# The second tile's last 512 output columns go as two quarters in two PSUM banks, and the first batch's gathered columns in three

## The chip, the cores and the metric

The kernel runs on one core of a Trainium2 chip. A core has a matrix engine (TensorE, here PE, with its weight loads shown apart as PEld), a vector engine (DVE), a scalar engine (ACT), a general-purpose engine (GpSimd, here POOL), a sync engine (SP) that issues most DMAs, an on-chip memory (SBUF) and eight accumulation banks of 128 x 512 float32 (PSUM). Each engine runs its own instructions in the order written and waits for others on semaphores. The metric is the device time of one execution in microseconds. Before the change the median of three runs is 1198.57 us (1197.81 to 1199.47).

## The reference

Two layers over 256 tokens of width 1024, all in float32. Each layer is a mixer of three attentions with one output projection, and then a mixture of experts in which every token goes to 2 of 64 experts. Cut to what matters here:

```python
def reference(x, ...):
    for l in range(DEPTH):                                   # DEPTH = 2
        mix = hybrid_mixer(x, ...)                           # ..., return o @ w_out
        x = layer_norm(ALPHA * x + mix, ln1_g[l], ln1_b[l])
        ffn = moe_ffn(x, router_w, router_b, moe_w1[l], moe_w3[l], moe_w2[l])
        x = layer_norm(ALPHA * x + ffn, ln2_g[l], ln2_b[l])

def route(xf, router_w, router_b):                           # 64 experts in 8 groups of 8
    s = sigmoid(xf @ router_w); sb = s + router_b
    # the group with the largest sum of its best two, then its best two experts
    return e_idx, s_sel / s_sel.sum(-1, keepdims=True)

def moe_ffn(...):   # per expert e, over its tokens xb
    hb = silu(xb @ w1[e]) * (xb @ w3[e]);  y = hb @ w2[e]    # 1024 -> 256 -> 1024, gated sum per token
```

## The kernel before, in words

The 256 tokens are two tiles (t = 0, 1) of 128 rows; `x[:, t, :]` holds a tile. The experts are worked through in 16 batches of four, with 32 slots of tokens for each expert. The weights of all 64 experts are read in each layer, whatever the routing: 12 DMAs of 1 MB for a batch (two for w1 and w3 of each expert, `load_w13`, line 344, and one for w2, `load_w2`, line 348), into two sets of buffers, `w_even` and `w_odd`. SP issues them in written order and waits before each for the buffer's last reader. A w1/w3 buffer is free when the batch has multiplied it (`part_psum`, line 417), the four w2 buffers when the batch's second product is done (`y2_psum`, line 423 and line 431).

This case is about the stretch between the attention and the first batch, once in each layer. In order:

- PE multiplies the attention outputs `oT` by `w_out` (`out_chunk`, line 672): for tile t and half h of the 1024 columns eight matmuls of 512 columns into `mix_bank[t][h]` (banks 0 to 3), and `mix_psum` after the eighth.
- DVE adds each half to the residual and takes its statistics (`add_mix`, line 1141: a SCALAR_TENSOR_TENSOR at line 1144, BN_STATS at 1146), with the signal `z_ready`; `moments` (line 1148) closes the tile, POOL takes the power for the standard deviation (line 475).
- PE turns the sums around (`transpose_z`, line 570), ACT copies them to `xT` (`copy_xT`), and PE multiplies them by the router's weights (`route`, line 794).
- DVE selects the experts (`scores`, `select`, signal `picked`), PE counts ranks (lines 826 to 858), DVE places the tokens (`place`, line 1215, signal `chosen_ok`).
- PE gathers the normalised rows of the first batch by one-hot matmuls (`gather_first`, line 840): chunks 0 to 3 of eight into bank 2, 4 to 7 into bank 3. DVE copies bank 2 to `xg` with scale and offset (line 1277, four of 128 columns), ACT copies bank 3 (line 1513, four), and the first batch begins: for each expert k, PE multiplies chunks 0 to 3 after `xg_dve` and 4 to 7 after `xg_act` (lines 876 to 892). Expert 2 needs bank 0 back, so it waits for DVE's copy of expert 0 (line 1294, `part_dve`).
- Meanwhile the layer norm of x itself is finished: DVE does tile 0 by `center_first` (line 1156) and `stretch` (line 1165), one 512-column SCALAR_TENSOR_TENSOR per half each, with signal `x0_ready`; POOL does tile 1 in two multiplies and two adds (lines 519 and 523), with signal `x1_ready`, beginning after `routed`, DVE's last step of routing. ACT copies both to the banks `Y` (`seed`).

DVE, in written order around the gathered copies: `select(1)`, the stretch of half 0, `place(1)`, the number of rounds (lines 1268 to 1271), `weigh_scores(1)`, the stretch of half 1, the four copies of line 1277, `weights(1)` (lines 1205 to 1207), `weigh(0)` (lines 1233 and 1236), then the first batch.

Of the kernel before, what the change touches and what calls it, by code (L numbers as in the profile page):

```python
# [19 lines left out]
P = 128  # L20
# [59 lines left out]
def program(nc, a, consts, const_at, out):  # L80
# [17 lines left out]
    with ctx:  # L98
# [129 lines left out]
        class Signal:  # L228
# [23 lines left out]
        xT_psum, xT_dve, xT_act = Signal("xT_psum", 8), Signal("xT_dve", 3), Signal("xT_act", 7)  # L252
# [10 lines left out]
        mix_psum = Signal("mix_psum", 4)  # L263
# [5 lines left out]
            Signal("z_ready", 4), Signal("n_ready", 2), Signal("y_bits_set", 4), Signal("y_seeded", 4))  # L269
# [4 lines left out]
        chosen_ok, xg_dve, xg_act = Signal("chosen_ok"), Signal("xg_dve"), Signal("xg_act")  # L274
        gathered = Signal("gathered_first_half"), Signal("gathered_second_half")
# [47 lines left out]
        def _(sp):  # L323
# [3 lines left out]
            for l in range(DEPTH):  # L327
# [27 lines left out]
                if l == 0:  # L355
# [26 lines left out]
                sp.dma_start(router.rearrange("p (h c) e -> p h (c e)", h=2),  # L382
                             a["router_w"].rearrange("(h p c) e -> p h (c e)", h=2, c=4)).then_inc(router_in.sem, 16)
                sp.dma_start(router_bias, a["router_b"].partition_broadcast(P)).then_inc(router_in.sem, 16)
                for v, name in enumerate(("ln1_g", "ln1_b")):
                    sp.dma_start(g_cols[:, v, :], a[name].rearrange("l (p c) -> l p c", c=DC)[l]).then_inc(cols_in.sem, 16)
                    sp.dma_start(r_cols[:, v, :].rearrange("p (h c) -> p h c", h=2),
                                 a[name].rearrange("l (h p c) -> l p h c", h=2, c=4)[l]).then_inc(cols_in.sem, 16)
# [19 lines left out]
                after(sp, l, mix_psum, 4)  # L408
# [57 lines left out]
        def _(pool):  # L466
# [5 lines left out]
            for l in range(DEPTH):  # L472
# [65 lines left out]
        def _(pe):  # L538
# [16 lines left out]
            for l in range(DEPTH):  # L555
# [14 lines left out]
                def transpose_z(t, h):  # L570

                    after(pe, l, z_ready, 2 * t + h + 1)
                    zc = x[:, t, h * 512:(h + 1) * 512].rearrange("p (d c) -> p c d", c=4)
                    for c in range(4):
                        last = nc.tensor.transpose(bank[2 * t + h][:, c * P:(c + 1) * P], zc[:, c, :], ident)
                    last.then_inc(xT_psum.sem, 1)

# [216 lines left out]
                def route(t, h):  # L794
                    after(pe, l, xT_act, 3 + 2 * t + h + 1)
                    if t == 1 and h == 0:
                        after(pe, l, z_lin, 1)
                    for c in range(4 * h, 4 * h + 4):
                        last = mm(bank[0][:, t * NE:(t + 1) * NE], xT[:, c, t * P:(t + 1) * P], router[:, c, :],
                                  start=c == 0, stop=c == DC - 1)  # L800
                    if h == 1:
                        last.then_inc(z_psum.sem, 1)
# [9 lines left out]
                transpose_z(0, 0)  # L812
                transpose_z(0, 1)
# [7 lines left out]
                for c in range(5):  # L821
                    out_chunk(1, 1, c)
# [735 lines left out]
```

## Time and profile before

| | before |
|---|---|
| median of the runs | 1198.57 us |
| the profiled execution | 1198.07 us, span 1196.1 us |
| mean granted clock of TensorE | 0.986 |
| PE / PEld / DVE / ACT / POOL busy | 89% / 50% / 31% / 16% / 3% |
| chain that ended last, by engine | PE 47%; SPq 35%; DMA 8%; DVE 4%; issue 3%; ACT 1% |
| read from HBM | 441.16 MB, 370 GB/s over the span |

The page cuts the span into 40 equal slices of 29.9 us; a digit is the busy share in tenths:

```profile
PE   8999988899899888888899999899899889888885
DVE  2244462222232222122251535422232222222224
PEclk9999999999999999989999999999999999998998
DMA  9966389999999999999998456899999999999996
GB/s 353 345 222 246 141 322 420 420 420 420 421 421 421 420 421 421 421 420 420 396 350 319 149 216 245 338 418 421 421 421 421 421 421 420 420 420 421 421 420 235
```

Layer 0 fills slices 0 to 19, layer 1 the rest. The stretch of this case lies at 127 to 190 us, in slices 4 to 6, and at 717 to 780 us in layer 1. From there to the end of each layer DMA runs at one rate, 420 GB/s. A busy share is an average; what a change is worth is read from the waits at its place.

### The profile page before, as it was taken

How to read it: one execution, taken by the hardware profiler on the slowest of the kernel's cores; microseconds unless marked ns; L12 is line 12 of the kernel's file. 1: busy time of each engine (PE TensorE's matmuls, PEld its weight loads, DVE VectorE, ACT ScalarE, POOL GpSimd, SP SyncE). 2: the span in 40 equal slices, each digit the busy share in tenths (PEclk: the TensorE clock that was granted, in tenths of full speed). 3: DMA queues.
4: the chain of work that ended last, by engine and by line, in shares of the span. 5: the costliest groups of instructions: out<-in, count | busy, mean ns of one | idle time of the engine just before them, and what ended most of it. 6: DMA issues, size and time to landing. Idle time of an engine off the chain costs nothing.

```text
span 1196.1 us, 16270 instructions
## 1 busy us (share of the span) xinstructions
PE 1070.3 (89%) x6084; PEld 594.7 (50%) x6088; DVE 373.9 (31%) x1007; ACT 196.3 (16%) x469; POOL 34.0 (3%) x46
## 2 busy tenths in 40 slices
PE   8999988899899888888899999899899889888885
PEld 5565555444455444444356656544455444444442
DVE  2244462222232222122251535422232222222224
ACT  1144121111111111011122441211111111100110
POOL 0010020000000000000000100100000000000001
PEclk9999999999999999989999999999999999998998
DMA  9966389999999999999998456899999999999996
GB/s 353 345 222 246 141 322 420 420 420 420 421 421 421 420 421 421 421 420 420 396 350 319 149 216 245 338 418 421 421 421 421 421 421 420 420 420 421 421 420 235
DMA packets 85026, 442.68 MB, mean 370 GB/s; under 512 B 11009, under 2 KB 26497, under 8 KB 36865
## 3 DMA queue, kind: packets, MB, share of 16 engines
q1 hardware_dynamic: 84704, 441.60, 91.3%
q0 software_dynamic: 144, 0.58, 0.1%
q8 instruction: 20, 0.33, 0.1%
q14 instruction: 14, 0.11, 0.0%
q10 hardware_dynamic: 144, 0.07, 0.0%
HBM read 441.16 MB, written 1.05 MB: 370 GB/s over the span
## 4 chain that ended last, share of the span: by engine, by line
PE 47%; SPq 35%; DMA 8%; DVE 4%; issue 3%; ACT 1%; DVEq 0%; POOL 0%
SPq L344 24%; PE bank L602 12%; SPq L348 11%; PE bank L871 8%; PE bank L890 7%; DMA w_odd<-in_moe_w 7%; PE bank L680 5%; PE bank L922 4%; PE bank L927 4%; DMA w_odd<-in_w_in 2%; PE bank L897 1%; ACT moe L1366 1%; PE bank L650 1%; PE bank L665 1%; DVE moe L1320 1%
## 5 line engine op out<-in xcount | busy, mean ns | idle before, releaser
L871 PE MATMUL bank<-moe,x 128*128 128x128 f32 x960 | 233.1, 402 | 0.0
L871 PEld LDWEIGHTS bank<-moe,x 128*128 128x128 f32 x960 | 230.8, 335 | 0.0
L1366 ACT ACTIVATE moe<-bank 128x512 f32<-128x512 f32 (+2 forms) x190 | 101.4, 543 | 750.1 <-PE bank L890 361.0
L602 PE MATMUL bank<-w_odd 128*128 128x384 f32 (+1 forms) x448 | 150.9, 493 | 4.8 <-DMA w_odd<-in_w_in 2.9
L927 PE MATMUL bank<-moe 128*128 128x512 f32 x256 | 118.4, 605 | 24.1 <-DVE moe L1320 24.1
L890 PE MATMUL bank<-w_even,moe 128*32 128x512 f32 x1024 | 118.7, 609 | 17.1 <-DMA w_even<-in_moe_w 13.1
L890 PE MATMUL bank<-w_odd,moe 128*32 128x512 f32 x1024 | 118.0, 606 | 14.0 <-DMA w_odd<-in_moe_w 14.0
L1294 DVE COPY moe<-bank 128x512 f32<-128x512 f32 x64 | 44.2, 691 | 248.4 <-PE bank L890 248.1
L602 PEld LDWEIGHTS bank<-w_odd 128*128 128x128 f32 x448 | 83.6, 190 | 63.6 <-issue 14.2
L927 PEld LDWEIGHTS bank<-moe 128*128 128x128 f32 x256 | 46.0, 190 | 98.9 <-DVE moe L1320 51.4
L890 PEld LDWEIGHTS bank<-w_even,moe 128*32 128x32 f32 x1024 | 30.9, 111 | 100.0 <-issue 72.2
L890 PEld LDWEIGHTS bank<-w_odd,moe 128*32 128x32 f32 x1024 | 31.0, 111 | 95.7 <-issue 75.7
L922 PE MATMUL bank<-w_even,moe 128*32 128x512 f32 x512 | 58.3, 594 | 14.0 <-DVE moe L1311 14.0
L922 PE MATMUL bank<-w_odd,moe 128*32 128x512 f32 x480 | 54.8, 595 | 9.6 <-DVE moe L1311 9.6
L897 PE MATMUL bank<-moe,constants 128*32 128x512 f32 x256 | 35.8, 629 | 25.8 <-ACT moe L1366 25.8
L680 PE MATMUL bank<-w_odd 128*128 128x512 f32 x128 | 58.4, 599 | 0.0
L1305 DVE RECIPROCAL moe<-moe 128x256 f32<-128x256 f32 x32 | 56.1, 1753 | 1.1
L1320 DVE COPY moe<-bank 128x512 f32<-128x512 f32 x32 | 22.1, 692 | 109.3 <-PE bank L922 109.3
L1304 DVE TENSOR_SCALAR moe<-moe 128x256 f32<-128x256 f32 x32 | 9.4, 294 | 142.8 <-ACT moe L1525 142.8
L1366 ACT ACTIVATE w_odd<-bank 128x384 f32<-128x384 f32 (+3 forms) x74 | 32.5, 472 | 119.9 <-PE bank L602 34.5
L1311 DVE COPY moe<-bank 128x256 f32<-128x256 f32 x32 | 13.6, 425 | 101.6 <-PE bank L912 101.6
L922 PEld LDWEIGHTS bank<-w_even,moe 128*32 128x32 f32 x512 | 18.1, 109 | 42.7 <-issue 42.7
(160 smaller groups left out, 684.6 us busy)
## 6 DMA issues: line engine op xcount, KB each, us to landing
w_even<-in_moe_w SPq DMA_DIRECT2D x192, 1024.0 KB, 26.1
w_odd<-in_moe_w SPq DMA_DIRECT2D x184, 1024.0 KB, 26.4
w_odd<-in_w_in SPq DMA_DIRECT2D x24, 768.0 KB, 6.4
w_odd<-in_w_out SPq DMA_DIRECT2D x4, 2048.0 KB, 10.3
w_odd<-in_moe_w SPq DMA_DIRECT2D x16, 512.0 KB, 16.8
w_odd<-in_w_in SPq DMA_DIRECT2D x4, 832.0 KB, 10.9
w_odd<-in_ln_g SPq DMA_DIRECT2D x4, 512.0 KB, 7.9
w_odd<-in_ln_b SPq DMA_DIRECT2D x4, 512.0 KB, 8.7
```

What stands on the lines that cost most here:

```text
L344: sp.dma_start(w13_slots[parity][k][:, m, :, :].rearrange("p c f -> p (c f)"), w[l * NE + e * NB + k]).then_inc(w13_in[parity][k].sem, 16)
L348: sp.dma_start(w2_slots[parity][k].rearrange("p c d -> p (c d)"), w2[l * NE + e * NB + k]).then_inc(w2_in[parity][k].sem, 16)
L602: last = mm(h_bank[b][t][:, 0:n], xT[:, c, t * P:(t + 1) * P], w[:, c, :], start=c == 0, stop=c == DC - 1)
L680: last = mm(mix_bank[t][h][:, :], oT[:, c, t * P:(t + 1) * P], w_out_half[h][:, c, :], start=c == 0, stop=c == DC - 1, skip_group_check=True)
L871: last = mm(bank[2 + c // 4][:, c % 4 * P:(c % 4 + 1) * P], xc[:, t, c, :], chosen[:, t, :], start=t == 0, stop=t == 1)
L890: last = mm(bank[k % 2][BLK * q:BLK * (q + 1), :], xg[:, c, BLK * k:BLK * (k + 1)], w[:, :, c, :], start=c < 4, stop=c >= 4)
L897: last = mm(bank[0][BLK * k:BLK * (k + 1), :], const("fold"), partial[:, k, :], start=True, stop=True)
L922: last = mm(bank[2 + h][BLK * k:BLK * (k + 1), :], hT[:, c, BLK * k:BLK * (k + 1)], w2_slots[parity][k][:, c, h * 512:(h + 1) * 512], star ...
L927: return mm(Y[t][h][:, :], scatter[:, t * P:(t + 1) * P], y_rows[:, h * 512:(h + 1) * 512], start=False, stop=True, skip_group_check=True)
L1294: nc.vector.tensor_copy(partial[:, k, :], bank[k % 2][:, :]).then_inc(part_dve.sem, 1)
L1305: blink(nc.vector.reciprocal(eg, eg))
L1366: return fn(dst, src, ACT.Copy)
```

## The change

Three things change, in both layers.

1. The last 512 output columns of tile 1 are computed as two quarters of 256 columns, in bank 3 and bank 6, each with its own `mix_psum`, sum, statistics and `z_ready` on DVE (`add_quarter`). Each quarter is turned around by two transposes (banks 3 and 7) and copied by ACT on its own. The router's weights and its norm columns are laid out by quarters to match. PE's order around them changes.
2. The gathered columns of the first batch lie in three banks: chunks 0 to 3 in bank 2, 4 and 5 in bank 3, 6 and 7 in bank 1. ACT copies only 4 and 5; DVE copies 6 and 7 after its first four, and gives `xg_act` itself.
3. On DVE `center_first(0)` moves behind `select(1)` and `center_first(1)` behind the rounds, in the places that the two stretches had; both stretches move behind DVE's last gathered copy. POOL's rows of tile 1 wait for `rows_go`, the copy of chunk 6, in place of `routed`. On ACT, `seed(0)` moves behind its gathered copies.

```diff
@@ SP, router weights and columns by quarters
-                sp.dma_start(router.rearrange("p (h c) e -> p h (c e)", h=2),
-                             a["router_w"].rearrange("(h p c) e -> p h (c e)", h=2, c=4)).then_inc(router_in.sem, 16)
+                sp.dma_start(router.rearrange("p (q c) e -> p q (c e)", q=4),
+                             a["router_w"].rearrange("(q p c) e -> p q (c e)", q=4, c=2)).then_inc(router_in.sem, 16)
...
-                after(sp, l, mix_psum, 4)
+                after(sp, l, mix_psum, 5)
                 load_w13(1, 0, 1)
                 load_w2(1, 1, 1)
@@ POOL
-                after(pool, l, xT_psum, 8)
+                after(pool, l, xT_psum, 9)
                 after(pool, l, n_ready, 2)
                 after(pool, l, ln_in[0], 32)
-                after(pool, l, routed, 1)
+                after(pool, l, rows_go, 1)
@@ PE
+                def transpose_quarter(q):
+                    after(pe, l, z_ready, q + 2)
+                    transpose_z(1, q, (bank[3], bank[7])[q - 2]).then_inc(xT_psum.sem, 1)
...
+                def out_quarter(q, c):
+                    last = mm((bank[3], bank[6])[q - 2][:, 0:256], oT[:, c, P:2 * P],
+                              w_out_half[1][:, c, (q - 2) * 256:(q - 1) * 256],
+                              start=c == 0, stop=c == DC - 1, skip_group_check=True)
+                    if c == DC - 1:
+                        last.then_inc(mix_psum.sem, 1)
...
                 out_chunk(1, 0, 7)
-                for c in range(5):
-                    out_chunk(1, 1, c)
-                transpose_z(1, 0)
+                for c in range(DC):
+                    out_quarter(2, c)
+                transpose_half(1, 0)
+                out_quarter(3, 0)
                 rank = bank[1]
                 after(pe, l, picked, 1)
...
-                out_chunk(1, 1, 5)
-                out_chunk(1, 1, 6)
-                out_chunk(1, 1, 7)
-                route(1, 0)
+                for c in range(1, 5):
+                    out_quarter(3, c)
+                transpose_quarter(2)
+                for c in range(5, DC):
+                    out_quarter(3, c)
+                route(1, range(4), 6)
+                route(1, (4, 5), 7)
                 set_bits(0, 0)
-                transpose_z(1, 1)
-
+                transpose_quarter(3)
                 set_bits(0, 1)
-                route(1, 1)
+                route(1, (6, 7), 8)
...
-                        last = mm(bank[2 + c // 4][:, c % 4 * P:(c % 4 + 1) * P], nc_[:, c, :], chosen[:, t, :],
-                                  start=t == 0 and c % 4 == 0, stop=t == 1, skip_group_check=True)
-                        if t == 1 and c % 4 == 3:
-                            last.then_inc(gathered[c // 4].sem, 1)
+                        to, o = (bank[2], c * P) if c < 4 else (bank[3], (c - 4) * P) if c < 6 else (rank, (c - 4) * P)
+                        last = mm(to[:, o:o + P], nc_[:, c, :], chosen[:, t, :],
+                                  start=t == 0 and c in (0, 4), stop=t == 1, skip_group_check=True)
+                        if t == 1 and c in (3, 5, 7):
+                            last.then_inc((gathered[0] if c == 3 else first_mid if c == 5 else gathered[1]).sem, 1)
@@ DVE
                 weights(0)
-                center_first(0)
-                link(add_mix(1, 1))
-                moments(1, 5, LN_EPS)
-                center_first(1)
+                link(add_quarter(2))
+                link(add_quarter(3))
+                moments(1, 5, LN_EPS, 3)
                 scores(1)
                 select(1)
-                stretch(0, 0, x0_ready, (0,))
+                center_first(0)
...
                 weigh_scores(1)
-                stretch(0, 0, x0_ready, (1,))
+                center_first(1)
...
                 last.then_inc(xg_dve.sem, 1)
+                v.wait_ge(gathered[1].sem, b0 + 1)
+                after(v, l, first_mid_sb, 1)
+                for c, sig in ((6, rows_go), (7, xg_act)):
+                    ts(xg[:, c, :], bank[1][:, (c - 4) * P:(c - 3) * P], g_cols[:, 0, c:c + 1], g_cols[:, 1, c:c + 1],
+                       ALU.mult, ALU.add).then_inc(sig.sem, 1)
+                stretch(0, 0, x0_ready)
                 weights(1)
                 weigh(0, b0)
@@ ACT
-                act.wait_ge(gathered[1].sem, b0 + 1)
-                for c in range(4):
+                after(act, l, first_mid, 1)
+                for c in range(2):
...
-                last.then_inc(xg_act.sem, 1)
+                last.then_inc(first_mid_sb.sem, 1)
+                seed(0)
                 seed(1)
```

PE's instructions from the last 512-column matmul of tile 1's first half to the router's matmuls, before (bank3 and bank6 take the last 512 columns, 128x64 rows at L799 are the router's, at L826 and L828 the ranks):

```order
L680 MATMUL bank2<-w13_odd,w2_odd 128x512
L680 MATMUL bank3<-w13_odd,w2_odd 128x512 [waits s_masked]
L680 MATMUL bank3<-w13_odd,w2_odd 128x512 x4
L575 MATMUL bank2<-constants,x 128x128 [waits z_ready]
L575 MATMUL bank2<-constants,x 128x128 x3
L826 MATMUL bank1<-moe,constants 128x64 [waits picked]
L828 MATMUL bank1<-moe,constants 128x64
L680 MATMUL bank3<-w13_odd,w2_odd 128x512 x3
L799 MATMUL bank0<-moe,w2_odd 128x64 [waits z_lin,xT_act]
```

and now (L692 is the old L680, L807 the quarters, L576 the transposes, L846 and L848 the ranks, L818 the router):

```order
L692 MATMUL bank2<-w13_odd,w2_odd 128x512
L807 MATMUL bank3<-w13_odd,w2_odd 128x256 x8
L576 MATMUL bank2<-constants,x 128x128 [waits z_ready]
L576 MATMUL bank2<-constants,x 128x128 x3
L807 MATMUL bank6<-w13_odd,w2_odd 128x256
L846 MATMUL bank1<-moe,constants 128x64 [waits picked]
L848 MATMUL bank1<-moe,constants 128x64
L807 MATMUL bank6<-w13_odd,w2_odd 128x256 x4
L576 MATMUL bank3<-constants,x 128x128 [waits z_ready]
L576 MATMUL bank3<-constants,x 128x128
L807 MATMUL bank6<-w13_odd,w2_odd 128x256 x3
L818 MATMUL bank0<-moe,w2_odd 128x64 [waits z_lin,xT_act]
```

Between the last 512-column matmul of bank 2 and the first wait on `z_ready` there were five matmuls of 512 columns, and now there are eight of 256; a second wait on `z_ready` stands inside the last quarter.

DVE's instructions around the gathered copies, before (L1165 are the stretches, L1277 the gathered copies, L1207 to L1236 `weights` and `weigh`):

```order
L1202 TENSOR_TENSOR moe<-moe 128x64 [waits routed]
L1165 SCALAR_TENSOR_TENSOR x<-x,small,w2_odd 128x512 [waits pow_out,dve_step]
L1277 TENSOR_SCALAR moe<-bank2,small 128x128 [waits gathered_first_half,norm_columns_in]
L1277 TENSOR_SCALAR moe<-bank2,small 128x128 x3
L1205 TENSOR_REDUCE small<-moe 128x1
L1206 RECIPROCAL small<-small 128x1 [waits dve_step]
L1207 TENSOR_SCALAR moe<-moe,small 128x64 [waits dve_step]
L1233 TENSOR_TENSOR moe<-moe 128x128 [waits dve_step]
```

and now (L1185 is `center_first(1)`, L1305 and L1311 the gathered copies, L1194 the two stretches):

```order
L1231 TENSOR_TENSOR moe<-moe 128x64 [waits routed]
L1185 SCALAR_TENSOR_TENSOR x<-x,small,w2_odd 128x512 [waits n_ready,ln1_scales_in,xT_psum,dve_step]
L1305 TENSOR_SCALAR moe<-bank2,small 128x128 [waits gathered_first_half,norm_columns_in,dve_step]
L1305 TENSOR_SCALAR moe<-bank2,small 128x128 x3
L1311 TENSOR_SCALAR moe<-bank1,small 128x128 [waits first_batch_mid_sb,gathered_second_half]
L1311 TENSOR_SCALAR moe<-bank1,small 128x128
L1194 SCALAR_TENSOR_TENSOR x<-x,small,w2_odd 128x512 [waits pow_out]
L1194 SCALAR_TENSOR_TENSOR x<-x,small,w2_odd 128x512
L1234 TENSOR_REDUCE small<-moe 128x1
L1235 RECIPROCAL small<-small 128x1 [waits dve_step]
L1236 TENSOR_SCALAR moe<-moe,small 128x64 [waits dve_step]
L1262 TENSOR_TENSOR moe<-moe 128x128 [waits dve_step]
```

Two copies and both stretches now stand between the first four copies and `weights`, where nothing stood.

## Rows read from the trace of the kernel before

**Rows 1.** Windows: length, busy us by engine, PEclk, DMA share, GB/s

```profile
165.00:167.00 2.00, 1.39 (x16) 0.18 (x8) 0.18 (x1) 0.63 (x2) 0.00 (x0) 1.00 0.51 111
220.00:240.00 20.00, 17.50 (x114) 10.80 (x107) 6.33 (x13) 3.12 (x6) 0.00 (x0) 1.00 1.01 420
...
755.30:757.30 2.00, 0.85 (x8) 0.00 (x0) 1.05 (x3) 0.60 (x1) 0.00 (x0) 1.00 0.59 233
```

**Rows 2.** Timeline of SP: start us, us, engine, line, operation, count

```profile
164.80 7.97 SPq L344 DMA_DIRECT2D w_even<-in_moe_w  x8
...
186.54 1.75 SPq L348 DMA_DIRECT2D w_even<-in_moe_w  x4
...
775.88 1.75 SPq L348 DMA_DIRECT2D w_even<-in_moe_w  x4
```

**Rows 3.** Timeline of PE, ACT, output and router matmuls (two records for one matmul)

```profile
139.93 5.37 PE L680 MATMUL bank<-w_odd 128*128 128x512 f32 x12
145.14 0.74 PE L575 MATMUL bank<-constants,x 128*128 128x128 f32 x4
146.11 2.79 PE L680 MATMUL bank<-w_odd 128*128 128x512 f32 x6
150.53 0.60 ACT L1366 ACTIVATE w_odd<-bank 128x512 f32<-128x512 f32 x1 [4.03 <-PE bank L575]
151.19 1.10 PE L799 MATMUL bank<-moe,w_odd 128*128 128x64 f32 x8 [0.47 <-ACT w_odd L1366]
```

**Rows 4.** Timeline of DVE over the same stretch

```profile
144.38 0.69 DVE L1144 SCALAR_TENSOR_TENSOR x<-x,bank 128x512 f32<-128x512 f32 x1
146.38 0.23 DVE L1218 SCALAR_TENSOR_TENSOR moe<-bank,moe 128x64 f32<-128x64 f32 x1 [0.58 <-PE bank L828]
147.67 0.25 DVE L1207 TENSOR_SCALAR moe<-moe,small 128x64 f32<-128x64 f32 x1
149.01 0.69 DVE L1144 SCALAR_TENSOR_TENSOR x<-x,bank 128x512 f32<-128x512 f32 x1 [0.29 <-PE bank L680]
152.39 0.28 DVE L1179 SCALAR_TENSOR_TENSOR moe<-bank,small 128x64 f32<-128x64 f32 x1
```

**Rows 5.** Timeline of PE, an earlier place: eight matmuls, half of 256 columns

```profile
45.24 2.78 PE L708 MATMUL bank<-w_odd 128*128 128x256 f32 x16
```

**Rows 6.** Timeline: the second gather, DVE's copies, the first batch's experts

```profile
157.83 4.18 PE L843 MATMUL bank<-moe 128*128 128x128 f32 x16 [0.36 <-DVE moe L1212]
160.60 1.35 DVE L1277 TENSOR_SCALAR moe<-bank,small 128x128 f32<-128x128 f32 x4
162.37 4.02 PE L890 MATMUL bank<-w_even,moe 128*32 128x512 f32 x32 [0.36 <-DVE moe L1277]
168.19 3.64 PE L890 MATMUL bank<-w_even,moe 128*32 128x512 f32 x32 [1.80 <-DVE moe L1294]
```

**Rows 7.** Timeline of POOL and DVE, tile rows beside each other

```profile
158.86 1.27 POOL L519 TENSOR_TENSOR x<-moe,w_odd 128x512 f32<-128x512 f32 x1 [6.88 <-DVE iters L1271]
160.09 1.72 POOL L519 TENSOR_TENSOR x<-moe,w_odd 128x512 f32<-128x512 f32 x1
161.89 1.27 POOL L523 TENSOR_TENSOR x<-x,w_odd 128x512 f32<-128x512 f32 x1
...
156.56 0.75 DVE L1165 SCALAR_TENSOR_TENSOR x<-x,small,w_odd 128x512 f32<-128x512 f32 x1
158.98 1.69 DVE L1165 SCALAR_TENSOR_TENSOR x<-x,small,w_odd 128x512 f32<-128x512 f32 x1
162.31 0.90 DVE L1207 TENSOR_SCALAR moe<-moe,small 128x64 f32<-128x64 f32 x1
163.25 1.29 DVE L1233 TENSOR_TENSOR moe<-moe 128x128 f32<-128x128 f32 x1
```

**Rows 8.** A later gap of PE: its timeline row, and a window there

```profile
490.36 3.51 PE L890 MATMUL bank<-w_even,moe 128*32 128x512 f32 x16 [2.98 <-DMA w_even<-in_moe_w]
...
491.00:492.00 1.00, 1.00 (x8) 0.20 (x4) 0.00 (x0) 0.00 (x0) 0.00 (x0) 0.50 1.02 426
```

More of the change, by code:

```diff
@@ L262, in program @@
         o_psum, o_sb = Signal("o_psum", PAIRS), Signal("o_sb", PAIRS)
[L263 removed]
+        mix_psum = Signal("mix_psum", 5)
         x0_ready, x1_ready = Signal("x0_ready", 2), Signal("x1_ready", 2)
@@ L792, in _, with route @@
                 out_chunk(0, 1, 7)
-                def route(t, h):
-                    after(pe, l, xT_act, 3 + 2 * t + h + 1)
-                    if t == 1 and h == 0:
+                def out_quarter(q, c):
[4 more added lines that the diff above has]
+                        last.then_inc(mix_psum.sem, 1)
+                def route(t, chunks, copied):
+                    after(pe, l, xT_act, copied)
+                    if t == 1 and chunks[0] == 0:
                         after(pe, l, z_lin, 1)
-                    for c in range(4 * h, 4 * h + 4):
+                    for c in chunks:
                         last = mm(bank[0][:, t * NE:(t + 1) * NE], xT[:, c, t * P:(t + 1) * P], router[:, c, :],
                                   start=c == 0, stop=c == DC - 1)
-                    if h == 1:
+                    if c == DC - 1:
                         last.then_inc(z_psum.sem, 1)
@@ L1139, in _, with add_part, add_quarter, moments @@
                 nc.vector.tensor_copy(logit_bias, bank[7][:, NE:2 * NE]).then_inc(logit_bias_ok.sem, 1)
-                def add_mix(t, h):
-                    cols = slice(h * 512, (h + 1) * 512)
-                    after(v, l, mix_psum, 2 * t + h + 1)
-                    signal(stt(out=x[:, t, cols], in0=x[:, t, cols], scalar=float(ALPHA), in1=mix_bank[t][h][:, :],
-                               op0=ALU.mult, op1=ALU.add), z_ready, 2 * t + h + 1)
-                    return nc.vector.bn_stats(stats[:, t, h, :], x[:, t, cols])
-                def moments(t, o, eps):
-                    link(nc.vector.bn_aggr(mean_var[:, t, :], stats[:, t, 0:2, :].rearrange("p i s -> p (i s)")))
+                def add_part(t, i, cols, source):
+                    after(v, l, mix_psum, 2 * t + i + 1)
+                    signal(stt(out=x[:, t, cols], in0=x[:, t, cols], scalar=float(ALPHA), in1=source,
+                               op0=ALU.mult, op1=ALU.add), z_ready, 2 * t + i + 1)
+                    return nc.vector.bn_stats(stats[:, t, i, :], x[:, t, cols])
+                def add_mix(t, h):
+                    return add_part(t, h, slice(h * 512, (h + 1) * 512), mix_bank[t][h][:, :])
+                def add_quarter(q):
+                    return add_part(1, q - 1, slice(q * 256, (q + 1) * 256), (bank[3], bank[6])[q - 2][:, 0:256])
+                def moments(t, o, eps, parts=2):
+                    link(nc.vector.bn_aggr(mean_var[:, t, :], stats[:, t, 0:parts, :].rearrange("p i s -> p (i s)")))
                     ts(ms[:, o:o + 1], mean_var[:, t, 1:2], eps, None, ALU.add).then_inc(pow_in.sem, 1)
@@ L1499, in _ @@
                 copy_xT(0, 0, 5)
+                copy_xT(0, 1, 6)
                 route(0)
                 copy_xT(1, 0, 7)
+                for q in (2, 3):
+                    after(act, l, xT_psum, 6 + q)
+                    copy(xT[:, 2 * q:2 * q + 2, P:2 * P],
+                         (bank[3], bank[7])[q - 2][:, 0:256].rearrange("p (c t) -> p c t", c=2)).then_inc(xT_act.sem, 1)
                 route(1)
                 m, b0 = start_batches(act, base, l)
-                seed(0)
                 def copy_gathered(g):
```

30 lines of the change are left out of this document (17 added, 13 removed).

## The prediction

> **What bounds the kernel now.** I read the windows first. From 220 us on, DMA is full at 420 GB/s [rows 1], and the slices of the page show this rate to the end of each layer. The weights of a layer are a fixed number of bytes, so a layer ends when that stream ends, and the stream's start and its holes are what a change here can move. In 165:167 it had moved 111 GB/s x 2 us = 0.22 MB, so at 420 GB/s it in effect began at 167 - 0.53 = 166.5 us; in layer 1 by the same sum (233 x 2 = 0.47 MB) at 757.3 - 1.1 = 756.2.
>
> Then I read SP's issues. The first w1/w3 buffer is given back by expert 0 of the first batch, at 164.80 [rows 2]: 1.7 us before the stream's start, which I take as the time from issue to data. SP then issues nine DMAs of 1 MB (eight w1/w3, one w2), 9.44 MB, 22.5 us of stream: work until 166.5 + 22.5 = 189.0. The next issue waits for the first batch's second product, at 186.54 [rows 2], so its data could flow from 188.2. **The spare time of this second gate is only 0.8 us**; in layer 1 it is 756.2 + 22.5 - (775.88 + 1.7) = 1.1 us. So two gates matter: the first expert's end (gate 1), and the end of the whole first batch (gate 2). Later gates have room: one batch is 12.6 MB, 30 us of stream, and PE needs about 26 us for one. The views of PE and DVE then say what either gate hangs on.
>
> **The change, part by part.**
>
> *The quarters.* A 512-column matmul takes (145.14 - 139.93)/6 = 0.87 us [rows 3], one of 256 columns 0.43: at the earlier place eight matmuls with 1536 columns together took 2.78 us, against 2.6 by this rate [rows 5]. The split costs nothing in itself. But the order loses time. PE reaches the first wait for `z_ready` after 0.87 + 8 x 0.43 = 4.3 us, at 144.25, while DVE's sum, behind `select(0)`, begins only at 144.38 and ends at 145.07 [rows 4]. Before, exactly enough matmuls lay in front; now PE stands still for 0.9 us. Then one quarter matmul goes ahead of the ranks, so DVE's placing, at 146.38 before [rows 4], starts at 146.8, its `weights` end at 148.35 for 147.92, and the first quarter's sum follows at 148.4. That sum takes between 0.35 and 0.69 us (half and all of a 512-column one, [rows 4]); I take 0.42. PE has meanwhile done five quarter matmuls (146.1 to 148.3), waits until 148.85, turns two blocks in 0.35 (half of the four in 0.74, [rows 3]) and does the last three quarters in 1.3: the projection ends at 150.45. It ended at 148.95, as DVE's next sum at 149.01 shows [rows 4]. So 1.5 us later.
>
> The tail after it gets shorter. Before: 149.01 to DVE's logits at 152.39, 3.4 us. After: six router matmuls at 0.24 (the 1.10 of four less an end of 0.15, [rows 3]) = 1.45, one bit-setting matmul and two transposes 0.5, ACT's copy of 256 columns 0.4 (0.60 for 512, [rows 3]), two router matmuls and the hops 0.7: 3.05. The logits come 1.5 - 0.35 = 1.1 us later; bounds -0.3 (no stalls) and +1.5. POOL's power is hidden, as it was. `center_first(0)` takes the stretch's place behind `select(1)`, of the same length, but the wait behind it adds 0.1.
>
> *Gate 1.* Before: the gather ended at 162.0, PE began at 162.37 and expert 0 ended some 0.2 before 164.80 [rows 2, 6]; in it PE waited 0.3 for ACT's chunks. The three banks take that 0.3 away: ACT has two copies, DVE's two are done 0.9 us after the gather, and PE needs 0.4 + 0.9 to come to chunk 4. So gate 1 moves by 1.1 + 0.1 - 0.3 = +0.9 us (-0.6 to +1.3), and so does the stream's start. SP's loads into `w_odd`, 1.5 us later, still end near 162, before it.
>
> *Gate 2.* Expert 2 starts at 168.19, after a wait of 1.80 for DVE's copy of expert 0 [rows 6]. DVE sets this gate, and DVE is where the change adds. The gather now ends at 163.2. The copies of chunks 6 and 7 follow, in 0.34 steps (1.35 for four, [rows 6]), to 164.05. Chunk 6 releases POOL, whose multiply runs from 163.85. DVE then comes to the two stretches. Free, one takes 0.75; the one that met POOL took 1.69 [rows 7]. The rows show how: POOL ran 158.86 to 160.13, DVE's stretch from 158.98 ended at 160.67, about 0.55 behind POOL's end, and POOL's next took 1.72 for 1.27. L1207 too (0.25 in tile 0, [rows 4]) ended only 0.05 after a POOL row did, and L1233 took 1.29 beside the next. So each waits for the other's current instruction, and I lay them out in turns:
>
> - POOL's first multiply ends at 165.1, stretch 0 at 165.7.
> - POOL's second ends at 166.9, stretch 1 at 167.4.
> - POOL's first add ends at 168.6, L1207 at 168.65.
> - POOL's second add ends at 169.85, the first L1233 at 169.95, `weigh` with its second product and last step at 170.3.
>
> Before, `weigh` ended at 164.8 (163.25 + 1.29, another short product and a last step, [rows 7]). That is +5.45 us. Without any contention the same instructions would end at 164.05 + 1.5 + some 1.45 for `weights` and `weigh` (an estimate: six short steps of about L1207's free 0.25) = 167.0, +2.2. I take +5.45, since both ways of meeting POOL are in the rows; below 2.2 only if the quarters lose nothing, +1.1. What queues behind on DVE is its loop entry, the choice for batch 1 and the copy of expert 0; the one waiting is PE. ACT's seeds wait for the stretches and POOL too, but end at about 170.4, while expert 3 needs its copy of expert 1 only at 175: hidden.
>
> The Trainium skill, in "GPSIMD Engine Reference", section "Specifications", says that GpSimd shares its SBUF interfaces with VectorE and that the contention comes with vector instructions of two SBUF inputs or in a two-port mode. The trace agrees: 1.69 against 0.75 for a stretch, none for the four PSUM copies at 1.35. By it the rule speaks against this order, as it moves both two-input stretches from POOL's idle time into its rows.
>
> *PE's clock in the gap.* Between experts 1 and 3 PE would now stand from 167.3 to 173.65, 6.3 us for 1.8. After a gap of 2.98 us the 16 records of an expert took 3.51 us, with the granted clock at 0.50, the lower level of 1.2 GHz [rows 8]; 32 records took 3.64 at the full clock [rows 6], so 16 take 1.82, and the loss is 1.6. The gap of 1.80 cost nothing. I add 1.6 (0 to 1.9). Ahead of experts 0 and 1 nothing of the kind is added.
>
> **The sum.** Gate 2 goes from 186.54 to 186.54 + 5.45 + 1.6 = 193.6, its data from 195.3, where the stream before went on at 189.0: +6.3 us. In layer 1: 775.88 + 7.05 + 1.7 = 784.6 against 778.7, +5.9. The +0.9 of gate 1 lies inside this, since the hole follows it. Room after the first batch absorbs the rest, and the ends move with the stream: 12.2 us. 1198.07 of the profiled execution + 12.2 = 1210.3. That execution is 0.5 below the median of the runs shown, so I predict 1210.5.
>
> The router weights in four runs and smaller column pieces I cost at nothing: POOL, who uses them, is busy 3% of the span and done long before this stretch, and if they landed late the loss would be in the wait for the router's sums, not here. The wait for `mix_psum` 5 has the cover named above. `x0_ready` is needed by PE's next gather, which itself waits behind gate 2's chain.
>
> **The rivals.**
>
> - *No lower clock in the gap.* The dip comes not at all or is over by then. For it: the kernel has gaps without one. Against: the one long gap in the rows had it, and this one is twice as long. +4.7 + 4.3 = 9.0: 1207.
> - *The turns with POOL are milder.* If DVE goes first or holds on, `weigh` ends at about +2.2; the hole is then 2.2 - 0.8 = 1.4 and 1.1, and 2.5 in all: 1200.6; with part of the clock loss, as PE's gap would be 3.5 us, up to 1204. For it: one meeting at the end of a POOL row cost 0.05. Against: the release of POOL 0.2 us ahead of the stretch puts it first.
> - *Faster: the projection's tail decides.* If the quarters stall less than I lay out (the sum of the first half of tile 1 is early, or the ranks don't delay DVE), the logits come 0.3 earlier and the chunks' 0.3 adds: gate 1 is 0.6 earlier. It pays only if gate 2 has as much more room, that is if the stream has over 1 us of spare more than worked out and DVE's part is hidden: -1.2 in both layers, 1197. It decides where `weigh` ends less than 0.8 after its old time. Against: two stretches free of POOL alone are 1.5.
> - *Nothing shows.* `weigh` 1 us late, inside the spare: 1198 to 1200.
>
> **How the numbers follow.** Full turns and the lower clock 0.47 (1207.5 to 1213, as the clock's part and the quarters' stall vary); no lower clock 0.17; milder turns 0.20, of which a quarter is within the bound of telling; nothing shows 0.07; faster 0.09. About 0.2% (2.4 us) is what a measurement of this kernel tells from no change. So slower by more: 0.47 + 0.17 + 0.15 = 0.79; within: 0.05 + 0.07 = 0.12; faster: 0.09. The range leaves out half of the faster case and the nothing case, and the upper end: 1199 to 1213.
>
> **What would show it.** In the changed profile: PE idle ahead of the first transposes of tile 1 (0.9 us) and of the quarter's (0.5), and the logits near 153.5. SP's first L344-like issue into `w_even` near 165.7. The two stretches at over 1.2 us each, with POOL's rows at 1.3 to 1.7 between them. Expert 2 near 173.6 with PE's clock at 0.5 behind it. The w2 issue near 193.6 for 186.54, and windows from 190 to 195 us with an idle DMA, which were full. I am wrong if these windows are full, if the stretches run in 0.75, or if the logits come no later than 152.4.

## The result, and the profile after

The changed kernel took 1212.99 us (median of 4 runs, 1211.05 to 1213.46); the kernel before took 1199.02 beside it. The ratio is 1.0111 [1.0091, 1.0131]: **1.1% slower**, 13.3 us by the ratio. The profiled execution took 1213.11, its span is 1210.6 (+14.5) and its mean clock 0.981 (0.986 before).

On the page the loss is a hole in the stream. This is the line of GB/s by slices of 30.3 us:

```profile
GB/s 346 344 219 243 139 304 363 420 420 421 421 421 421 420 421 420 420 420 420 397 348 321 153 202 237 334 352 421 420 420 421 421 420 420 421 420 420 421 419 236
```

Slices 6 and 26, counted from 0 as in the profile before, hold 363 and 352 where 420 and 418 stood. SP's timeline (start us, us, then what) shows why, beside [rows 2]:

```profile
166.75 14.32 SPq L346 DMA_DIRECT2D w_even<-in_moe_w  x8
181.17 0.39 SPq L350 DMA_DIRECT2D w_odd<-in_moe_w  x1
194.84 1.97 SPq L350 DMA_DIRECT2D w_even<-in_moe_w  x4
...
791.45 1.98 SPq L350 DMA_DIRECT2D w_even<-in_moe_w  x4
```

Gate 2 opens at 194.84 for 186.54, and at 791.45 for 775.88. The eight w1/w3 issues now take 14.32 us for 7.97: the later ones wait for expert 2, which is late itself. The windows (columns as in [rows 1]) hold both holes:

```profile
178.00:181.00 3.00, 2.18 (x24) 0.36 (x20) 0.69 (x1) 0.60 (x1) 0.00 (x0) 0.90 0.69 216
190.00:192.00 2.00, 1.14 (x14) 0.43 (x17) 0.90 (x4) 0.60 (x1) 0.00 (x0) 1.00 1.02 426
192.00:197.00 5.00, 4.20 (x32) 1.49 (x25) 1.18 (x3) 0.60 (x1) 0.00 (x0) 1.00 0.23 67
```

Against 420 GB/s the holes lose (420 - 216) x 3 / 420 = 1.5 us and (420 - 67) x 5 / 420 = 4.2. With 1.3 for the later gate 1 (below) that is 7.0 us in layer 0. PE's first work of layer 1 began at 603.84, and before at 596.35: +7.5 us, of which 0.6 had been there before this stretch (tile 0's logits, on DVE):

```profile
140.85 0.28 DVE L1208 SCALAR_TENSOR_TENSOR moe<-bank,small 128x64 f32<-128x64 f32 x1 [5.34 <-PE bank L818]
...
603.84 1.05 PE L550 MATMUL bank<-constants 128*128 128x128 f32 x8
```

and the same two instructions in the kernel before:

```profile
140.21 0.28 DVE L1179 SCALAR_TENSOR_TENSOR moe<-bank,small 128x64 f32<-128x64 f32 x1 [5.35 <-PE bank L799]
...
596.35 1.05 PE L548 MATMUL bank<-constants 128*128 128x128 f32 x8
```

Times of layer 0 are therefore compared below **counted from tile 0's logits**.

What makes gate 2 late stands in DVE's and POOL's timelines, from the copy of chunks 6 and 7 (L1311) on:

```profile
164.16 0.73 DVE L1311 TENSOR_SCALAR moe<-bank,small 128x128 f32<-128x128 f32 x2 [0.46 <-PE bank L867]
164.81 1.76 DVE L1194 SCALAR_TENSOR_TENSOR x<-x,small,w_odd 128x512 f32<-128x512 f32 x1
166.49 1.77 DVE L1194 SCALAR_TENSOR_TENSOR x<-x,small,w_odd 128x512 f32<-128x512 f32 x1
...
168.62 0.81 DVE L1236 TENSOR_SCALAR moe<-moe,small 128x64 f32<-128x64 f32 x1
169.47 1.28 DVE L1262 TENSOR_TENSOR moe<-moe 128x128 f32<-128x128 f32 x1
...
164.74 1.28 POOL L521 TENSOR_TENSOR x<-moe,w_odd 128x512 f32<-128x512 f32 x1 [11.36 <-DVE moe L1311]
...
167.79 1.59 POOL L525 TENSOR_TENSOR x<-x,w_odd 128x512 f32<-128x512 f32 x1
```

The stretches take 1.76 and 1.77 us for 0.75, L1236 0.81 for 0.25. Each ends just behind the POOL instruction in progress (the stretches 0.55 behind, L1236 0.05 behind), as in [rows 7]; I read this as DVE waiting for POOL's current instruction, and short_pool_rows below tests it. Then PE's timeline, and windows over its gap and what follows:

```profile
164.46 3.86 PE L914 MATMUL bank<-w_even,moe 128*32 128x512 f32 x32
...
174.42 5.70 PE L914 MATMUL bank<-w_even,moe 128*32 128x512 f32 x32 [6.09 <-DVE moe L1328]
```

```profile
173.00:174.00 1.00, 0.00 (x0) 0.00 (x0) 0.82 (x3) 0.00 (x0) 0.00 (x0) 0.50 1.01 426
174.42:180.10 5.68, 5.68 (x32) 1.21 (x32) 0.69 (x1) 0.00 (x0) 0.00 (x0) 0.63 0.85 319
```

PE stands for 6.1 us, the granted clock is then at 0.50, the lower level of 1.2 GHz, and the 32 records take 5.70 us where [rows 6] had 3.64. In layer 1 they take 6.41.

### The profile page after: what moved, and what is told of

It is laid out like the page before. It is cut to its first block, busy times and chain, and to the rows that moved or that the text cites. A ratio compares the mean times of both kernels' runs of the same rounds, so it can differ in the third digit from the quotient of the medians.

```text
span 1210.6 us, 16344 instructions
## 1 busy us (share of the span) xinstructions
PE 1075.8 (89%) x6120; PEld 600.4 (50%) x6120; DVE 378.2 (31%) x1015; ACT 195.5 (16%) x467; POOL 33.5 (3%) x46
## 3 DMA queue, kind: packets, MB, share of 16 engines
HBM read 441.16 MB, written 1.05 MB: 365 GB/s over the span
## 4 chain that ended last, share of the span: by engine, by line
PE 48%; SPq 35%; DMA 6%; DVE 6%; issue 3%; ACT 1%; DVEq 0%; POOL 0%
SPq L346 23%; SPq L350 12%; PE bank L614 11%; PE bank L895 8%; PE bank L914 8%; PE bank L946 4%; PE bank L951 4%; PE bank L692 3%; DMA w_even<-in_moe_w 2%; DMA w_odd<-in_moe_w 2%; DMA w_odd<-in_w_in 2%; PE bank L921 1%; ACT moe L1400 1%; PE bank L662 1%; PE bank L677 1%
## 5 line engine op out<-in xcount | busy, mean ns | idle before, releaser
L914 PE MATMUL bank<-w_even,moe 128*32 128x512 f32 x1024 | 123.4, 630 | 22.8 <-DMA w_even<-in_moe_w 11.6
L946 PE MATMUL bank<-w_even,moe 128*32 128x512 f32 x512 | 59.9, 609 | 13.9 <-DVE moe L1345 13.9
L692 PE MATMUL bank<-w_odd 128*128 128x512 f32 x96 | 44.2, 600 | 0.0
```

The lines of the kernel that those rows point to most:

```text
L692: last = mm(mix_bank[t][h][:, :], oT[:, c, t * P:(t + 1) * P], w_out_half[h][:, c, :], start=c == 0, stop=c == DC - 1, skip_group_check=True)
L914: last = mm(bank[k % 2][BLK * q:BLK * (q + 1), :], xg[:, c, BLK * k:BLK * (k + 1)], w[:, :, c, :], start=c < 4, stop=c >= 4)
L946: last = mm(bank[2 + h][BLK * k:BLK * (k + 1), :], hT[:, c, BLK * k:BLK * (k + 1)], w2_slots[parity][k][:, c, h * 512:(h + 1) * 512], star ...
```

## The experiments

The theory is the prediction's: gate 2 decides, and it is late by (a) the quarters, (b) the two stretches behind the copies, (c) DVE and POOL in turns, (d) PE's lower clock. The main rival is that the stretches cost by themselves, or the clock nothing. This is what each run gave. The last five columns are from layer 0 of the profiled execution: when DVE takes up tile 1's router sums (its logits), when `weigh` ends, how long PE stands before expert 2, how long the 32 records of experts 2 and 3 take, and when gate 2 opens. The times of logits, `weigh` and gate 2 are counted from tile 0's logits. A ratio is to executions of the kernel before that ran beside that kernel; their median was 1199.02 us beside the change, 1199.29 beside the two tuned_more kernels and 1199.78 beside the others. Diffs are against the changed kernel where nothing else is said.

| kernel | median us | ratio to before | tile 1's logits | `weigh` ends | PE's gap | experts 2, 3 | gate 2 |
|---|---|---|---|---|---|---|---|
| before | 1199.02 | | 12.18 | 24.62 | 1.80 | 3.64 | 46.33 |
| the change | 1212.99 | 1.0111 [1.0091, 1.0131] | 13.41 | 30.18 | 6.09 | 5.70 | 53.99 |
| quarters_only | 1203.94 | 1.0033 [1.0023, 1.0044] | 14.21 | 26.63 | 1.85 | 3.64 | 48.35 |
| banks_and_order_only | 1208.83 | 1.0068 [1.0051, 1.0084] | 12.19 | 28.96 | 6.31 | 5.48 | 52.53 |
| old_dve_order | 1207.85 | 1.0057 [1.0041, 1.0074] | 14.21 | 28.50 | 3.50 | 5.27 | 51.50 |
| short_pool_rows | 1202.77 | 1.0026 [1.0014, 1.0038] | 13.42 | 26.60 | 2.22 | 3.64 | 48.33 |
| pool_at_routed | 1208.25 | 1.0076 [1.0056, 1.0096] | 13.41 | 27.85 | 3.07 | 5.34 | 51.27 |
| peeled | 1214.60 | 1.0124 [1.0103, 1.0145] | 13.41 | 30.19 | 5.58 | 6.22 | 54.51 |
| peeled_warm | 1208.10 | 1.0079 [1.0061, 1.0096] | 13.41 | 30.20 | warm | 3.64 | 51.93 |
| tuned_three_banks | 1199.97 | 1.0004 [0.9993, 1.0014] | 12.30 | 24.96 | 2.06 | 5.34 | 48.03 |
| tuned_more_three_banks | 1198.95 | 0.9991 [0.9981, 1.0001] | 11.99 | 24.47 | 1.68 | 3.64 | 46.20 |
| tuned_more_two_banks | 1199.57 | 1.0003 [0.9991, 1.0014] | 11.99 | 24.49 | 1.90 | 3.64 | 46.20 |

### The parts alone

**quarters_only**: the quarters stay; banks, DVE's order, POOL's release and ACT's seed are as before.

```diff
@@ DVE
+                center_first(0)
                 link(add_quarter(2))
                 link(add_quarter(3))
                 moments(1, 5, LN_EPS, 3)
+                center_first(1)
...
@@ POOL
-                after(pool, l, rows_go, 1)
+                after(pool, l, routed, 1)
```

> The kernel before with the quarters alone: PE's new order, add_quarter on DVE, the router by quarters; gathered columns in two banks, DVE's order around the copies and POOL's start as before. Theory A (the quarters lose 1.2 us in each layer because PE stands at two z_ready waits, and the rest of the loss is DVE's stretches beside POOL): logits of tile 1 some 1.2 us later than before, weigh and the first batch's end later by the same 1.2, weights stream 1.2 us later and no new hole; 2.4 us slower than before, about 1201.5. Rival B (the quarters carry the loss, by PE's order): over 7 us slower. Rival C (the quarters gain, the banks and the order lose all): 1 to 2 us faster than before.

It is 4 us slower (0.33%). DVE and PE around the first quarter's sum (L1166), each from its own timeline:

```profile
148.30 0.75 DVE L1184 SCALAR_TENSOR_TENSOR x<-x,small,w_odd 128x512 f32<-128x512 f32 x1
149.09 0.42 DVE L1166 SCALAR_TENSOR_TENSOR x<-x,bank 128x256 f32<-128x256 f32 x1
...
149.57 0.50 PE L576 MATMUL bank<-constants,x 128*128 128x128 f32 x2 [1.18 <-DVE x L1166]
```

With `center_first(0)` ahead of the sum, the transposes wait 1.18 us for DVE; in the full change 0.39. So the new place of `center_first(0)` helps the quarters: the logits are 2.03 late here (and in old_dve_order, with the same order), 1.23 in the change. 2.4 us were expected in all. The loss goes through gate 1, which is 1.98 later; gate 2 is 2.02 later, and 1.2 of that is above its spare of 0.8.

**banks_and_order_only**: the other half of the change, with the 512-column projection of before; this diff is against the kernel before.

```diff
@@ DVE
                 scores(1)
                 select(1)
-                stretch(0, 0, x0_ready, (0,))
+                center_first(0)
...
                 last.then_inc(xg_dve.sem, 1)
+                for c, sig in ((6, rows_go), (7, xg_act)):
+                    ts(xg[:, c, :], bank[1][:, (c - 4) * P:(c - 3) * P], g_cols[:, 0, c:c + 1], g_cols[:, 1, c:c + 1],
+                       ALU.mult, ALU.add).then_inc(sig.sem, 1)
+                stretch(0, 0, x0_ready)
                 weights(1)
```

> The kernel before with whole halves, and parts 2 and 3 alone: three banks, DVE's copies of chunks 6 and 7, both stretches behind them, POOL released by chunk 6. Theory A: the first expert ends about 0.2 us earlier, weigh ends 4.4 us later than before, PE's gap between experts 1 and 3 is about 5 us and the granted clock falls there (2 us more), the first batch ends 6.3 us later, a hole of some 5.5 us in the stream in each layer: 11 us slower than before, about 1210. Rival B (the quarters carry the loss): within 3 us of before.

8.2 us slower by the ratio, with logits on time (12.19); 11 were expected. Gate 2 came as late as expected (+6.20 for +6.3), and the span of the profiled execution is 9.8 longer than that of before. The gap and the clock are there in full, and DVE's stretches together take this:

```profile
162.76 3.46 DVE L1167 SCALAR_TENSOR_TENSOR x<-x,small,w_odd 128x512 f32<-128x512 f32 x2
```

So 4.0 and 8.2 make 12.2 of 13.3. That the parts nearly add is in part chance: alone the quarters lose at gate 1, while in the full change their smaller delay of 1.23 adds to gate 2's.

### DVE's order and POOL

**old_dve_order** keeps quarters, banks and `rows_go`, and puts DVE's centerings and stretches where they were. The diff shows the stretches and one centering.

```diff
+                stretch(0, 0, x0_ready, (0,))
...
                 weigh_scores(1)
-                center_first(1)
+                stretch(0, 0, x0_ready, (1,))
...
-                stretch(0, 0, x0_ready)
                 weights(1)
```

> The changed kernel with DVE's centers and stretches back in the places of before (the quarters, the three banks, DVE's copies of chunks 6 and 7 and POOL's late start stay). Theory A: behind the copies DVE has only weights and weigh, which meet two of POOL's rows, so weigh ends near 167.8 instead of 171.0 in layer 0, expert 2 starts 3.2 us earlier, the first batch ends 3.2 us earlier or 5 if the low clock in PE's gap goes too: 1203 to 1207. Rival (the stretches are covered, the late release of POOL itself is the cost through x1_ready): no change from the changed kernel, 1213.

It gives back half only, 1207.85 where 1203 to 1207 was expected: `weigh` ends 1.7 us earlier than in the change, not 3.2. The stretches are gone from behind the copies, but POOL's rows still begin there, and `weights` and `weigh` meet them (its L1262 and L1265):

```profile
165.18 0.83 DVE L1236 TENSOR_SCALAR moe<-moe,small 128x64 f32<-128x64 f32 x1
166.04 1.50 DVE L1262 TENSOR_TENSOR moe<-moe 128x128 f32<-128x128 f32 x2
167.47 1.23 DVE L1265 TENSOR_SCALAR moe<-moe 128x8 f32<-128x8 f32 x1
```

**short_pool_rows** is the test of the turns: the change with POOL's four rows shortened to 8 columns of each half. It leaves out tile 1's layer norm for the other columns; each engine still has the same instructions in the same order.

```diff
-                    cols = slice(h * 512, (h + 1) * 512)
+                    cols = slice(h * 512, h * 512 + 8)
```

> The changed kernel, but POOL's four rows of tile 1 work on 8 columns of each half only, so tile 1's layer norm is left out for the other columns. Theory A (DVE's stretches and weigh wait in turns for POOL's instructions): the two stretches take 1.5 us together instead of 3.45, weights and weigh 1.5 instead of 2.9, weigh ends near 167.8 in layer 0, 3.2 us earlier, and the time is 1203 to 1207. Rival (the stretches would be slow without POOL, or their delay is covered): the stretches stay near 3.4 us, or the time stays at 1213.

```profile
163.78 1.40 DVE L1194 SCALAR_TENSOR_TENSOR x<-x,small,w_odd 128x512 f32<-128x512 f32 x2
...
165.54 0.26 DVE L1236 TENSOR_SCALAR moe<-moe,small 128x64 f32<-128x64 f32 x1
165.83 0.49 DVE L1262 TENSOR_TENSOR moe<-moe 128x128 f32<-128x128 f32 x2
```

DVE's instructions and their order are the same, yet the two stretches take 1.40 for 3.45, and `weigh` ends 3.6 earlier. 10 of the 13.3 us are back. **The turns with POOL, and what they bring about at the clock, are about three quarters of the loss**; the stretches' own 1.5 us of work is small beside them. POOL's end also comes earlier here, and with it ACT's copies of `x`. That path was not the last one: in the change ACT copies expert 1's result at 171.50, behind those copies, and PE begins expert 2 only at 174.42, when DVE releases it.

**pool_at_routed** is the change with POOL released by `routed` again.

```diff
-                after(pool, l, rows_go, 1)
+                after(pool, l, routed, 1)
```

> The changed kernel, with POOL's rows released by routed as before, in place of the copy of chunk 6. Theory A (what POOL's rows meet on DVE decides): POOL starts near 160.8 in layer 0, its multiplies meet center_first(1) and the first copies come at most 0.5 later; its adds meet the two stretches, and weights and weigh run free (1.5 us in place of 2.9). weigh ends 1.5 to 2 us earlier than in the changed kernel, 3 to 5 us in the whole time: 1208 to 1210. Rival (the late release is what saves time and the stretches alone cost): 1213 or more.

1.0076: some 4 us back, as expected. POOL now meets `center_first(1)` (1.69 us) and the first stretch, and is done before `weights`:

```profile
162.45 1.69 DVE L1185 SCALAR_TENSOR_TENSOR x<-x,small,w_odd 128x512 f32<-128x512 f32 x1
...
166.17 2.68 DVE L1194 SCALAR_TENSOR_TENSOR x<-x,small,w_odd 128x512 f32<-128x512 f32 x2
...
169.50 0.49 DVE L1262 TENSOR_TENSOR moe<-moe 128x128 f32<-128x128 f32 x2
```

### The clock

**peeled** writes the first two batches outside the loop, as a control; **peeled_warm** adds five matmuls of constants in PE's gap before expert 2, on a bank that is written anew later. The main lines of peeled_warm's diff are these; peeled has 0 in place of 5.

```diff
+                        if k == 2:
+                            for i in range(warm):
+                                mm(bank[3][:, :], ident, CT[:, 0:512], start=True, stop=True)
...
-                with pe.Fori(0, m, 2) as j:
+                batch(0, 0, False, 5)
+                batch(0, 1, False)
+                with pe.Fori(2, m, 2) as j:
```

> The changed kernel with PE's first two batches written out ahead of its loop; nothing else changes. A control for the next run: all theories expect the time of the changed kernel, 1213, and the granted clock at 0.50 behind the gap between experts 1 and 3.

> As the kernel peeled, with five more matmuls of 512 columns (4.3 us, into bank 3, which nobody reads then) ahead of PE's wait for expert 2 in the first batch of each layer. Theory A (the clock that falls in PE's gap is a term of the loss): experts 2 and 3 take 3.64 us in place of 5.70 and 6.41, the first batch ends 2.1 and 2.8 us earlier, and the time is 4 to 5 us shorter than that of peeled, about 1208. Rival (the hole in the stream is set by something else, or the clock falls all the same): within 1 us of peeled.

PE's timeline of peeled, and then of peeled_warm:

```profile
174.32 6.22 PE L917 MATMUL bank<-w_even,moe 128*32 128x512 f32 x32 [5.58 <-DVE moe L1333]
```

```profile
167.34 4.56 PE L908 MATMUL bank<-constants 128*128 128x512 f32 x10
173.73 3.64 PE L917 MATMUL bank<-w_even,moe 128*32 128x512 f32 x32 [1.83 <-DVE moe L1333]
```

`weigh` ends at the same place (30.19 and 30.20), but experts 2 and 3 take 3.64 for 6.22, gate 2 comes 2.6 earlier, and over the two layers 6.5 us come back against peeled by the medians, 5.4 by the ratios. Expected were 4 to 5. The traces give 5.6: in peeled experts 2 and 3 lose 2.6 and 3.0 us to the clock (6.22 and 6.61 for 3.64), more than the prediction's term. peeled is 1.6 above the change by the medians, and the intervals of the two ratios overlap.

### A version without PE's two stalls

**tuned_three_banks** keeps the quarters and the banks, and takes the two stalls out: two matmuls of the last quarter go ahead of the first wait, two router matmuls ahead of the last quarter's last one, and the first quarter's sum ahead of `place(0)`. DVE's other places and POOL's release are as before. The main lines on PE and the first move on DVE:

```diff
@@ PE
+                for c in range(2):
+                    out_quarter(3, c)
                 transpose_half(1, 0)
-                out_quarter(3, 0)
@@ DVE
                 link(add_mix(1, 0))
+                link(add_quarter(2))
                 signal(place(0), chosen_first, 1)
```

> Quarters in an order without stalls, two more quarter matmuls ahead of the first z_ready wait, the first quarter's sum on DVE ahead of place(0), two router matmuls ahead of the last quarter matmul; three banks; DVE's centers and stretches in the places of before and POOL released by routed as before. Theory A (PE's two stalls are what the quarters lose): tile 1's logits at 151.9 to 152.3 in layer 0, 0.1 to 0.5 us before those of the kernel before; the first expert 0.4 to 0.8 us earlier; weigh 0.2 to 0.5 later by the two copies, inside the 0.8 us of spare: 1197.5 to 1199.5. Rival (quarters lose by their number, in the extra sums and transposes, not by the stalls): over 1201.

Equal to before within what can be told. The logits were to come 0.1 to 0.5 us earlier than before and came 0.12 later. In layer 0 the lower clock followed a gap of 2.06 us, and gate 2 is later by just the 1.70 us that this costs (48.03 for 46.33):

```profile
169.09 5.34 PE L917 MATMUL bank<-w_even,moe 128*32 128x512 f32 x32 [2.06 <-DVE moe L1332]
```

**tuned_more_three_banks** also runs `center_first(1)` ahead of the last quarter's sum, as its POOL power (1.05 us) had met the centering, and both stretches are done at 157.97, before POOL's rows begin at 158.93; `weights(1)` goes ahead of the copies of chunks 6 and 7. **tuned_more_two_banks** is the same with the gathered columns in two banks. Against tuned_three_banks:

```diff
                 center_first(0)
+                center_first(1)
                 link(add_quarter(3))
                 moments(1, 5, LN_EPS, 3)
-                center_first(1)
...
                 v.wait_ge(chosen_ok.sem, b0 + 1)
+                stretch(0, 0, x0_ready, (1,))
...
-                stretch(0, 0, x0_ready, (1,))
...
                 last.then_inc(xg_dve.sem, 1)
+                weights(1)
                 v.wait_ge(gathered[1].sem, b0 + 1)
...
-                weights(1)
                 weigh(0, b0)
```

> As tuned_three_banks, and on DVE three moves: center_first(1) ahead of the last quarter's sum (so POOL's power meets no two-input instruction), the stretch of half 1 directly behind place(1), ahead of POOL's release, and weights(1) between the two groups of gathered copies. Theory A: POOL's power takes 0.55 us in place of 1.05 and the logits come 0.3 us earlier; the stretch takes 0.75 in place of 1.69; weigh ends about 1 us earlier than in tuned_three_banks, PE's gap stays under 2 us and the clock at 1.00; the first expert 0.3 us earlier. In all 0.5 to 1 us under the kernel before, 1197.5 to 1199.5. Rival (the order on DVE no longer matters once the stalls of PE are gone): equal to tuned_three_banks, 1200.

> The same quarters without stalls and the same places of the centers and stretches, but the gathered columns in two banks with four copies on ACT as before. Theory A: the logits as in the kernel with three banks; the first expert 0.3 us later than there, since PE waits for ACT's chunks; weigh 0.7 us earlier, with no DVE copies of chunks 6 and 7. 0 to 0.6 us under the kernel before, 1198 to 1200. Rival (three banks are worth more than 0.3 us a layer): over 1 us slower than the kernel with three banks.

```profile
167.67 3.64 PE L917 MATMUL bank<-w_even,moe 128*32 128x512 f32 x32 [1.68 <-DVE moe L1332]
```

Both have their logits 0.2 earlier and gate 2 0.1 earlier than before, and neither time can be told from the kernel before: 0.9991 [0.9981, 1.0001] and 1.0003 [0.9991, 1.0014]. 0.5 to 1 us of gain was expected with three banks. So with the two stalls taken out the idea is worth at most 0.2%, and the third bank shows no gain of its own. In layer 0 it had nothing to give: PE no longer waited for ACT in experts 0 and 1, but the granted clock was 0.50 over their first 1.23 us, and they took 4.22 us (1.06, a wait of 0.39 and 2.78 at the full clock with two banks). No version clearly beats the kernel before.

## Why the prediction was right

The forecast was 1210.5 within 1199 to 1213, slower at 0.79; 1212.99 was measured. That it lies inside the range at all is luck: it is 0.01 us from the upper end, and two of the four executions, the profiled one among them (1213.11), lie above it. By its own sum the forecast should have been 1210.8 (1210.3 and 0.5), not 1210.5. The way itself was the one laid out, step by step (layer 0, less the 0.64 that was there before):

- **The quarters.** PE's first stall was put at 0.9 us and is 0.66, as the brackets of PE's rows show; the second at 0.5, and is 0.39. The logits were to come +1.1 and came +1.23. Two misses cancel here: DVE's last sum began 1.76 later (151.41 - 149.01 - 0.64) for 1.5, and the tail behind it took 2.85 for 3.05.

```profile
145.77 0.74 PE L576 MATMUL bank<-constants,x 128*128 128x128 f32 x4 [0.66 <-DVE x L1167]
...
149.50 0.50 PE L576 MATMUL bank<-constants,x 128*128 128x128 f32 x2 [0.39 <-DVE x L1167]
```

- **Gate 1.** +0.9 predicted, 166.75 - 164.80 - 0.64 = +1.3 measured. The 0.3 for ACT's chunks did not come back in full: experts 0 and 1 took 3.86 for 4.02 us. PE no longer waits in them, but they began at the lower clock, where the prediction had added nothing; at the full clock throughout such records take 3.64 (peeled_warm). In layer 1 they took 4.26. The window over their start:

```profile
164.00:165.00 1.00, 1.00 (x6) 0.20 (x8) 0.84 (x3) 0.06 (x1) 0.26 (x1) 0.52 0.06 16
```

- **Gate 2, DVE's part.** +5.45 predicted, +5.57 measured at the end of `weigh`. The turns with POOL began 0.25 later than laid out (164.74 - 0.64 for 163.85) and took 6.30 for 6.45, so here too two small misses cancel; from POOL's start to the end of each stretch the layout is right to 0.1 us.
- **The clock.** +1.6 predicted, 5.70 - 3.64 = 2.06 measured, and 2.77 in layer 1. This is the mis-sized term. The estimate took only expert 2's half (16 records at the lower clock), from [rows 8], and its upper end was 1.9; in fact the clock was still low in expert 3. Its subtraction is also off: 3.51 - 1.82 is 1.69, not 1.6.
- **The sum.** 7.05 predicted for gate 2 and 7.66 measured; less the spare of 0.8, 6.9 of hole and delay, which the windows gave as 7.0. The profiled execution was forecast at +12.2 and is at +15.0. Of the 2.8 between, 0.6 is from before the stretch, 0.5 from outside the span, 0.6 from layer 0's clock and gate, and 1.1 from layer 1's, where the clock cost more. The ratio, over all runs, gives 13.3.

Of the rivals, "no lower clock in the gap" falls by peeled against peeled_warm; "milder turns" by DVE's rows and by short_pool_rows; "faster" and "nothing shows" by the ratio. What the prediction did not name is the first small hole at 178: it counted two gates only, and the one of expert 2's w1/w3 buffer, between them, is late too. It costs nothing more in the sum, because gate 2 ends later still.

The rule of the Trainium skill, "GPSIMD Engine Reference", section "Specifications", that GpSimd and VectorE contend for shared SBUF interfaces, held: 1.76 against 0.75 us for a two-input stretch beside POOL, while four copies out of PSUM took 1.35 beside POOL's rows in the kernel before and 1.36 in the changed kernel, where POOL stood still. L1236, with one tensor as input, was slowed as well (0.81 for 0.25); no run here shows by which part of the rule.

## What to carry to other kernels

Find the gates on which the stream of weights waits and how much spare each has, before judging the work between them: here 0.8 us of spare turned a delay of 7.7 us at one gate into a stream that ends 6.9 us later. Moving work "behind" a critical copy on an in-order engine puts it ahead of everything written after it, and here, where it then met POOL's rows, it cost over twice its length (1.76 us for 0.75). A split into smaller pieces needs the work before each wait re-counted, or the pieces arrive and stand.

## What the runs showed of the hardware that was not expected

- A gap of 2.06 us on PE was followed by the lower clock in tuned_three_banks (32 records in 5.34 us), and one of 1.93 in its layer 1 was not (3.64); in short_pool_rows a gap of 2.22 us was not (3.64), but 2.10 us in its layer 1 was (5.34). In layer 1 of pool_at_routed a gap of 2.56 us was not (3.64), and in layer 1 of tuned_three_banks, in the second product, one of 0.95 us was (5.33). So the length of the gap alone does not decide; what does is open.
- The loss does not grow with the gap in a simple way: gaps of 6.09, 5.58 and 5.07 us were followed by 5.70, 6.22 and 6.41 us for the same 32 records.
- POOL and DVE delay each other, but DVE pays far more here: with POOL's rows shortened `weigh` ended 3.6 us earlier, while POOL's four rows took 5.8 us in all beside DVE's stretches (2.97 and 2.81) and 5.06 in tuned_more_three_banks, with the stretches done before, so POOL lost 0.7. Short instructions pay too: `weigh`'s 128x8 step took 1.23 us in old_dve_order for 0.16.

```profile
164.74 2.97 POOL L521 TENSOR_TENSOR x<-moe,w_odd 128x512 f32<-128x512 f32 x2 [11.36 <-DVE moe L1311]
167.79 2.81 POOL L525 TENSOR_TENSOR x<-x,w_odd 128x512 f32<-128x512 f32 x2
```
